# S5 stage of an encoder layer: outputs of a channel tile delayed into the next turn, loops written out, rotations between low parts

## The chip, the cores and the metric

One core of a Trainium2 chip runs the whole program once. The metric is the device time of one execution in microseconds, and what counts is the median of the runs. The engines are PE (TensorE, matmuls), DVE (VectorE), ACT (ScalarE), POOL (GpSimd, here an issuer of DMAs) and SP (SyncE, an issuer of DMAs).

## The reference, cut to what matters

Two layers. Each projects x (256 tokens, 2048 channels) to many parts, runs three mixers on them (an S5 state-space scan with a gate, a Hyena convolution, latent attention), gates and lifts their outputs, projects and normalises. The change touches the S5 mixer, the first steps of attention, and one loop of the lift.

```python
def s5_mixer(u, ...):  # 256 tokens x 1024 channels
    y = uf * d
    for direction in range(2):
        bu = jnp.einsum('blgh,gph->blgp', uf, b_bar)
        _, state = lax.associative_scan(_linear_recurrence_op, (a, bu), axis=1, reverse=(direction == 1))
        y = y + jnp.real(jnp.einsum('blgp,ghp->blgh', state, c_mat))
    y = jax.nn.gelu(y.reshape(bsz, L, W_A))
    return y * jax.nn.sigmoid(y @ w_glu + b_glu)
...
q = (rms_norm(c_q, q_norm_g) @ w_uq).reshape(bsz, L, MLA_HEADS, dqk)
q = jnp.concatenate([q[..., :MLA_NOPE], apply_rope(q[..., MLA_NOPE:], pos)], axis=-1)
k_rope = apply_rope(k_r[:, :, None, :], pos)
```

## The kernel before, in words

**Weights.** All large matmuls run in two parts of fp32r. SP streams 184 blocks of weights (1 MB each) per layer into a ring of four half blocks. For each quarter of a block ACT copies a high part, `WH` (`make_wh`, L398, or `make_wh_quarter`, L404), DVE subtracts it from the raw weights to get the low part, `WL` (`make_wl_quarter`, L417, or `make_wl`, L426), and PE uses both. There is one `WH` and one `WL`, each of four quarters: a quarter can be made anew only when PE has used the old one (`parts_used`). A quarter of `WL` that isn't ready stops PE.

**The S5 stage.** It comes after eight "ax" blocks (the input of the mixer, evicted by ACT, completed by an addition on DVE, `add_input`, L645, sent through `u_scratch` in DRAM and back into `U4` by POOL, 8 DMAs for each of 8 tiles, L476). The stage has 8 turns, one per channel tile `ct`, as a loop (`Fori`) on each engine. PE runs, in a turn, the blocks 0 to 7 of the other projections (`block_at`, `wide_block`, matmuls of lines 1768 and 1770, 16 pairs per block, banks 0 and 1 in turn) and between them five groups of small matmuls:

- after block 1: `turn()` (L1810), transposes of the input matrices `E`, 16 records;
- after block 2: `inputs()` (L1830), 64 records, which need `UC`, the turn's copy of `U4` that ACT makes (L1396);
- after block 3: `lags()` (L1847, L1851), 40 records, which need `F` and `EZ`;
- after block 6: `direct()` (L1866), 16 records, which need `M`, the lags sent through `lag_scratch` by POOL (L488, L494);
- after block 7: `outputs()` (L1887), 64 records, which need the states `SP` that DVE has scanned, and `F`.

ACT evicts the sum of banks 6 and 7 to `Y4` (L1433), POOL sends it through `y_scratch` into `U4` (L498, L506, 8 DMAs). The order of each engine's work is written out by hand: DVE's low parts (`wl_for(j, q)`) and additions (`add_block(j)`, L746) stand between the steps of its own S5 work, ACT's high parts (`split_high(j)`) and evictions (`evict(j)`, L1371) between its own.

**Behind the stage.** ACT squares the latent projections in one instruction (`SQ`, L1439), PE sums them (L1915), ACT makes the eight gelus (L1443), two square roots (L1447), three silus (L1452) and, when PE has run the gate's matmuls (GLU, L1927), eight sigmoids (L1458) that free banks 0 to 3. DVE turns the roots into the normalised latents (L897 to L909), multiplies (L915, L921), and rotates the rotary parts (`rotate`, L927 to L929): that of k after the gate, that of q (4 tiles at once) before the low parts of the second V block. PE goes on with the q projection (L1943, 12 columns), k (8 columns) and V (L1972). The lift of the third branch is a loop of 2 turns of 12 blocks on PE (L2124), with `settle()` (drains that send what releases are pending, L1665) ahead of it and inside each turn.

The matmuls of this stage that wait on others do so by `take_bank` (a bank's last reader is done) and by waits on named semaphores; `ahead=` puts such waits before the last pair of a wide block.

Of the kernel before, what the change touches and what calls it, by code (L numbers as in the profile page):

```python
# [178 lines left out]
def trunk(nc, x, blocks, lp, ln, bc, w1, w2, b3, decay, feats, pT, pos, angles, consts, out):  # L179
    with ExitStack() as ctx:  # L180
# [83 lines left out]
        SQ = area(121, 8)  # L264
# [188 lines left out]
        def _(pool):  # L453
# [7 lines left out]
            for layer in range(DEPTH):  # L461
# [24 lines left out]
                with pool.Fori(0, WT) as ct:  # L486
# [16 lines left out]
                    for q in range(PAIRS):  # L503
                        for g_ in range(2):
                            rows = slice(32 * q + 16 * g_, 32 * q + 16 * g_ + 16)
                            pool.dma_start(split(U4[rows, bass.ds(ct * T, T)], STEP), by_group[q // 2, q % 2, g_]).then_inc(y_loaded, 16)  # L506
# [55 lines left out]
        def _(dve):  # L562
# [61 lines left out]
            for layer in range(DEPTH):  # L624
# [114 lines left out]
                with dve.Fori(0, WT) as ct:  # L739
                    st.enter(ct, DVE_S5_STEPS)  # L740
# [70 lines left out]
                    add_block(1)  # L811
# [76 lines left out]
                    st.leave(WT)  # L888
# [36 lines left out]
                def rotate(x, swapped, n, o):  # L925
                    cb, sb_ = (c.unsqueeze(1).to_broadcast([P, n, T]) for c in (cosr, sinr))
                    st.did(v.tensor_tensor(o, x, cb, ALU.mult))  # L927
                    st.did(v.tensor_tensor(swapped, swapped, sb_, ALU.mult)); st.wait()
                    v.tensor_tensor(o, o, swapped, ALU.add).then_inc(qk_ready, 1)  # L929
# [5 lines left out]
                rotate(PROJt[:, 32:33, :], PROJt[:, 33:34, :], 1, kt[:, 0:1, :])  # L935
# [19 lines left out]
                for i in range(2):  # L955
                    make_wl(dve, v, layer, lift_a(0) if i else B_V + 1)
# [368 lines left out]
        def _(act):  # L1325
# [11 lines left out]
            for layer in range(DEPTH):  # L1337
# [28 lines left out]
                with act.Fori(0, WT) as ct:  # L1366
                    st.enter(ct, ACT_S5_STEPS)
# [58 lines left out]
                    evict(6)  # L1426
                    split_high(7)
                    evict(7)
                    act.wait_ge(y4_free, layer * WT + (ct + 1))
                    for g in range(2):  # L1430
                        full(7 - g, "s5", ct)
                        into = Y4.rearrange("p (q g c) -> p q g c", q=2, g=2)[:, :, g, :]
                        free(a.activation(into, split(bank[7 - g][:, 0:P], 2), ACT.Copy), 7 - g)  # L1433
                    st.leave(WT)

                for b in (0, 1):
                    out_of(b, "s5", 31)

                a.activation(SQ, PROJ[:, 24 * T:32 * T], ACT.Square).then_inc(sq_ready, 1)  # L1439
                act.wait_ge(s_ready, layer * (2 * WT) + 2 * WT)  # L1440
                for ct in range(WT):
                    act.wait_ge(y_loaded, layer * (128 * WT) + 128 * (ct + 1))
# [918 lines left out]
```

## Time and profile before

| | us |
|---|---|
| median of the runs (2472.39, 2474.95, 11741.6) | 2474.95 |
| the profiled execution's own time | 2472.02 |
| its span, first to last instruction | 2470.4 |
| PE busy | 2407.2 |
| PE weight loads busy | 1993.0 |
| DVE busy | 1829.0 |
| ACT busy | 1226.3 |
| POOL busy | 251.2 |

The span is what the rows below divide up: their times run from its start. Layer 0 has its first matmul at 14.73, layer 1 at 1241.57. A matmul's busy time overlaps its neighbour's, so steps between starts tell more than lengths. "issue" is time in which an engine waited for nothing that the profile shows. PEclk is the granted clock of TensorE as a share of 2.4 GHz.

### The profile page before, as it was taken

The numbers are of one execution on the slowest core, as the hardware profiler recorded it, in microseconds if no ns is written. First come the engines' busy times: TensorE is split into PE (matmuls) and PEld (weight loads), VectorE is DVE, ScalarE is ACT, GpSimd is POOL, SyncE is SP. The second block draws the span as 40 slices with busy tenths as digits, with TensorE's granted clock in tenths as the row PEclk, the third lists the DMA queues.
The fourth block names the chain that finished last, engine by engine and source line by source line (L and its number), as shares of the span: only waits on it lengthen the run. The fifth ranks groups of instructions, "written<-read, shape, count | busy, mean of one in ns | idle before, by whom it ended". The sixth has DMA issues, their size and how long they took to land.

```text
span 2470.4 us, 42952 instructions
## 1 busy us (share of the span) xinstructions
PE 2407.2 (97%) x15144; PEld 1993.0 (81%) x15144; DVE 1829.0 (74%) x3195; ACT 1226.3 (50%) x2206; POOL 251.2 (10%) x486
## 2 busy tenths in 40 slices
PE   7999999999999999999989999999999999999998
PEld 6888888887777777898778888888877777788987
DVE  7888888677787776566678888886777777755655
ACT  5555555564543435453455555555654444444534
POOL 3321211100000000000052121121000000000000
PEclk9999999999999999999999999999999999999999
DMA  7555555455453435555565555554544534365553
GB/s 261 186 176 170 178 170 179 150 167 162 154 180 110 150 115 186 192 174 170 170 218 173 170 172 176 176 175 143 172 159 156 177 109 151 117 196 189 171 177 137
DMA packets 124696, 414.72 MB, mean 168 GB/s; under 512 B 19909, under 2 KB 26107, under 8 KB 124337
## 3 DMA queue, kind: packets, MB, share of 16 engines
q1 hardware_dynamic: 107136, 390.12, 47.8%
q0 software_dynamic: 17456, 23.23, 3.3%
q8 instruction: 65, 1.06, 0.2%
q14 instruction: 39, 0.31, 0.1%
HBM read 405.01 MB, written 7.21 MB: 167 GB/s over the span
## 4 chain that ended last, share of the span: by engine, by line
PE 93%; DVE 4%; issue 1%; ACT 1%; PEldq 0%; DMA 0%; PEld 0%; DVEq 0%; POOL 0%; ACTq 0%; POOLq 0%
PE bank L1726 31%; PE bank L1768 21%; PE bank L1770 10%; PE bank L2159 7%; PE bank L1701 5%; PE bank L2079 2%; PE bank L1927 2%; PE bank L1943 2%; PE bank L2093 1%; PE bank L2059 1%; PE bank L1683 1%; PE bank L1999 1%; PE bank L1830 1%; PE bank L1998 1%; PE bank L2041 1%
## 5 line engine op out<-in xcount | busy, mean ns | idle before, releaser
L398 ACT ACTIVATE WH<-ring 128x512 fp32r<-128x512 f32 x1376 | 861.6, 631 | 1105.9 <-PE bank L1726 461.3
L426 DVE TENSOR_TENSOR WL<-ring,WH 128x512 fp32r<-128x512 f32 x860 | 578.3, 689 | 401.1 <-ACT WH L398 398.2
L1768 PE MATMUL bank<-XX,WH 128*128 128x512 f32 x2304 | 830.3, 404 | 31.6 <-DVE XX L617 14.7
L1770 PE MATMUL bank<-XX,WL 128*128 128x256 f32 x2304 | 650.5, 282 | 0.0
L1768 PEld LDWEIGHTS bank<-XX,WH 128*128 128x128 f32 x2304 | 436.0, 189 | 142.4 <-issue 34.1
L1726 PE MATMUL bank<-WH,XX 128*128 128x512 f32 x1536 | 485.8, 398 | 5.0 <-issue 3.0
L417 DVE TENSOR_TENSOR WL<-ring,WH 128x512 fp32r<-128x512 f32 x556 | 380.2, 689 | 149.1 <-ACT WH L398 127.7
L1770 PEld LDWEIGHTS bank<-XX,WL 128*128 128x128 f32 x2304 | 439.6, 191 | 0.0
L1726 PEld LDWEIGHTS bank<-WH,XX 128*128 128x128 f32 x1536 | 285.3, 188 | 81.5 <-issue 21.9
L1726 PE MATMUL bank<-WL,XX 128*128 128x512 f32 x768 | 300.1, 391 | 0.0
L1726 PEld LDWEIGHTS bank<-WL,XX 128*128 128x128 f32 x768 | 144.3, 188 | 30.8
L1701 PE MATMUL bank<-XX,WH 128*128 128x256 f32 x640 | 115.9, 284 | 1.0 <-issue 1.0
L1701 PEld LDWEIGHTS bank<-XX,WH 128*128 128x128 f32 x640 | 99.8, 192 | 1.8 <-issue 1.8
L2159 PE MATMUL bank<-WH,MIXH 128*128 128x512 f32 x256 | 100.5, 393 | 0.0
L2159 PE MATMUL bank<-WL,MIXH 128*128 128x512 f32 x256 | 99.9, 390 | 0.0
L2159 PE MATMUL bank<-WH,MIXL 128*128 128x512 f32 x256 | 99.8, 390 | 0.0
L1701 PE MATMUL bank<-XX,WL 128*128 128x256 f32 x320 | 90.7, 284 | 0.0
L506 POOL DMA_DIRECT2D ARENA<-y_scratch x128 | 66.0, 516 | 81.5 <-DMA y_scratch<-ARENA 63.4
L494 POOL DMA_DIRECT2D ARENA<-lag_scratch x128 | 65.7, 513 | 78.0 <-DMA lag_scratch<-ARENA 52.2
L476 POOL DMA_DIRECT2D ARENA<-u_scratch x128 | 66.5, 528 | 0.2
L1701 PEld LDWEIGHTS bank<-XX,WL 128*128 128x128 f32 x320 | 61.5, 192 | 0.0
L2079 PE MATMUL bank<-ARENA,CON 128*128 128x512 f32 x128 | 57.5, 597 | 0.7 <-issue 0.6
(329 smaller groups left out, 3241.9 us busy)
## 6 DMA issues: line engine op xcount, KB each, us to landing
ring<-in_blocks SPq DMA_DIRECT2D x736, 512.0 KB, 3.3
ARENA<-in_bc POOLq DMA_DIRECT2D x2, 2048.0 KB, 9.0
ARENA<-in_decay POOLq DMA_DIRECT2D x8, 512.0 KB, 4.7
ARENA<-in_x SPq DMA_DIRECT2D x4, 512.0 KB, 7.2
u_scratch<-ARENA POOLq DMA_DIRECT2D x16, 128.0 KB, 3.4
ARENA<-u_scratch POOLq DMA_DIRECT2D x128, 16.0 KB, 3.3
ARENA<-lag_scratch POOLq DMA_DIRECT2D x128, 16.0 KB, 2.7
y_scratch<-ARENA POOLq DMA_DIRECT2D x16, 128.0 KB, 3.4
```

What stands on the lines that cost most here:

```text
L398: nc.scalar.activation(wh[q], raw(which[0], q), ACT.Copy).then_inc(wh_ready[q], 1)
L417: nc.vector.tensor_tensor(wl[q], raw(which[0], q), wh[q].bitcast(F32), ALU.subtract).then_inc(w_used[slot(which[0], q // 2)], 1)
L426: vec.tensor_tensor(wl[q], raw(which[0], q), wh[q].bitcast(F32), ALU.subtract).then_inc(w_used[slot(which[0], half)], 1)
L476: pool.dma_start(split(U4[rows, m * T:(m + 1) * T], 4), by_step[s_, t]).then_inc(u4_loaded, 16)
L494: pool.dma_start(split(M[rows, :], 4), by_half[s_][:, :, (STEP - 1 - t) * 16:(2 * STEP - 1 - t) * 16]).then_inc(m_ready, 16)
L506: pool.dma_start(split(U4[rows, bass.ds(ct * T, T)], STEP), by_group[q // 2, q % 2, g_]).then_inc(y_loaded, 16)
L1701: ins = mm(o, w_, x_, start=start and i == 0 and n == 0, stop=stop and i == 7 and n == 2)
L1726: ins = mm(bank[b][:, :], x_, w_[q], start=first and n == 0, stop=last and n == 2)
L1768: ins = mm(bank[b][:, :], h, xx[:, :, k, :], start=(k == 0), stop=(k == DT - 1), skip_group_check=True)
L1770: ins = mm(bank[b][:, 0:T], l, xh[:, k, :], start=False, stop=(k == DT - 1), skip_group_check=True)
L2079: ins = mm(bank[b][:, :], tab[:, t, m * P:(m + 1) * P], ZT[:, t * W + half * CW:t * W + (half + 1) * CW], start=(t == 0), stop=(t == 1))
L2159: ins = mm(bank[b][:, :], x_[:, k, token[t]], w_[q], start=False, stop=(k == 15 and n == 2), skip_group_check=True)
```

## The change

- PE, ACT, DVE and POOL run the 8 turns of the S5 stage as straight code, not as a loop; so does PE for the lift of the third branch, without its drains.
- On PE, `direct()` and `outputs()` of turn `ct` move into turn `ct + 1`, behind block 1, around `turn()`: direct of the turn before, turn of this one, outputs of the turn before. `inputs()` moves behind block 3, ahead of `lags()`. After the last turn: `direct()`, the sums of squares, `outputs()`.
- The wait for both "ax" additions ahead of the stage and the drains there go.
- ACT: the eviction to `Y4` moves with `outputs()`, behind `turned(1)` of the next turn; `UC` waits for `direct()` of the turn before, and in turn 0 for all U4 loads, not for the first tile's. The squares are eight instructions, four at the end of turn 4 and four at the end of turn 5, into eight scattered areas. The gelus 0 to 2 move ahead of the high parts of the last block.
- DVE: `add_block(1)` moves ahead of the first write of `F`, and that write waits for the matmuls of `outputs()` of the turn before.
- POOL: the y transfer of a turn goes behind block 1 of the next, ahead of its lag transfer.
- DVE: k's rotation goes between low parts of the second k block, q's between the first two low parts of the second V block.

```diff
@@ POOL
-                with pool.Fori(0, WT) as ct:
+                def spread_lags(ct):
...
+                def turn_outputs(ct):
...
+                for ct in range(WT):
+                    if ct:
+                        turn_outputs(ct - 1)
+                    spread_lags(ct)
+                turn_outputs(WT - 1)
@@ DVE
-                with dve.Fori(0, WT) as ct:
-                    st.enter(ct, DVE_S5_STEPS)
+                for ct in range(WT):
...
+                    add_block(1)
                     ft = [b[:, 0:40 * 16] for b in (T1, T2)]
                     for b in (6, 7):
-                        dve.wait_ge(psum_free[b], nth(layer, "s5", b, ct))
+                        if ct:
+                            full(b, "s5", ct - 1)
+                        else:
+                            dve.wait_ge(psum_free[b], nth(layer, "s5", b, ct))
...
-                    add_block(1)
...
-                rotate(PROJt[:, 32:33, :], PROJt[:, 33:34, :], 1, kt[:, 0:1, :])
...
                     make_wl_quarter(q, layer, after_k(4 + q))
+                    if q < 3:
+                        rotate(q, PROJt[:, 32:33, :], PROJt[:, 33:34, :], 1, kt[:, 0:1, :])
...
-                rotate(qr, qs, 4, qt)
+                rotate(0, qr, qs, 4, qt)
+                make_wl_quarter(0, layer, B_V + 1)
+                rotate(1, qr, qs, 4, qt)
+                make_wl_quarter(1, layer, B_V + 1)
+                rotate(2, qr, qs, 4, qt)
@@ ACT
+                def outputs_out(ct):
+                    act.wait_ge(y4_free, layer * WT + (ct + 1))
+                    for g in range(2):
+                        full(7 - g, "s5", ct)
+                        into = Y4.rearrange("p (q g c) -> p q g c", q=2, g=2)[:, :, g, :]
+                        free(a.activation(into, split(bank[7 - g][:, 0:P], 2), ACT.Copy), 7 - g)
...
-                    act.wait_ge(us_landed, layer * WT + WT)
-                    act.wait_ge(u4_loaded, layer * (128 * WT) + (ct * 128 + 128))
-                    a.activation(UC, U4[:, bass.ds(ct * T, T)], ACT.Copy).then_inc(uc_ready, 1)
+                    if ct == 0:
+                        act.wait_ge(us_landed, layer * WT + WT)
+                        act.wait_ge(u4_loaded, layer * (128 * WT) + 128 * WT)
+                    if ct:
+                        act.wait_ge(direct_done, layer * (2 * WT) + 2 * ct)
+                    a.activation(UC, U4[:, ct * T:(ct + 1) * T], ACT.Copy).then_inc(uc_ready, 1)
                     turned(0)
                     turned(1)
+                    if ct:
+                        outputs_out(ct - 1)
...
                     evict(6)
+                    if ct == WT - 1:
+                        act.wait_ge(s_ready, layer * (2 * WT) + 2 * WT)
+                        for k in range(3):
+                            gelu(k)
                     split_high(7)
                     evict(7)
...
+                    if 4 <= ct < 6:
+                        if ct == 4:
+                            for b in (0, 1):
+                                out_of(b, "s5", 15)
+                        for k in range(4 * ct - 16, 4 * ct - 12):
+                            a.activation(SQ[k], PROJ[:, (24 + k) * T:(25 + k) * T], ACT.Square).then_inc(sq_ready, 1)
+                outputs_out(WT - 1)
+                for k in range(3, WT):
+                    gelu(k)
...
-                a.activation(SQ, PROJ[:, 24 * T:32 * T], ACT.Square).then_inc(sq_ready, 1)
@@ PE
-                settle()
                 pe.wait_ge(consts_loaded, 16)
-                with pe.Fori(0, WT) as ct:
+                for ct in range(WT):
...
-                    for b in (0, 1):
-                        out_of(b, "ax", 3)
+                    def all_made():
+                        matrices_made()
+                        if ct:
+                            lags_spread(ct - 1)
+                            states_made(ct - 1)
                     block_at(0)
-                    block_at(1, matrices_made)
+                    block_at(1, all_made)
+                    if ct:
+                        direct()
                     turn()
-                    block_at(2, matrices_turned)
+                    if ct:
+                        outputs(ct - 1)
+                    block_at(2)
+                    block_at(3, matrices_turned)
                     inputs()
-                    block_at(3)
                     lags()
                     block_at(4)
                     block_at(5)
-                    block_at(6, lags_spread)
-                    direct()
-                    block_at(7, states_made)
-                    outputs()
+                    block_at(6)
+                    block_at(7, (lambda: lags_spread(WT - 1)) if ct == WT - 1 else None)
+                direct()
                 for i in range(2):
-                    pe.wait_ge(sq_ready, layer + 1)
+                    pe.wait_ge(sq_ready, layer * 8 + (4 * i + 4))
...
+                    if i == 0:
+                        states_made(WT - 1)
+                outputs(WT - 1)
...
-                settle()
-                with pe.Fori(0, 2) as turn:
-                    for j in range(12):
-                        if j == 4:
-                            pe.wait_ge(yl_ready, layer * 4 + 4)
-                        gated_block("lift", j // 6 + turn * 2, j % 6, (xh, xl), yb, B_LIFT + 48 + j, turn, 12)
-                    settle()
+                for j in range(24):
+                    if j == 4:
+                        pe.wait_ge(yl_ready, layer * 4 + 4)
+                    gated_block("lift", j // 6, j % 6, (xh, xl), yb, B_LIFT + 48 + j)
```

## Rows read from the trace of the kernel before

**Rows 1.** The page, part 1: busy us, share of the span, instructions
```profile
PE 2407.2 (97%) x15144; PEld 1993.0 (81%) x15144; DVE 1829.0 (74%) x3195; ACT 1226.3 (50%) x2206; POOL 251.2 (10%) x486
```

**Rows 2.** Waits of PE: for whom, total us, times, longest us
```profile
PE bank L1915 <- ACT ARENA L1439: 5.9, 2, 2.9
PE bank L1768 <- issue: 4.9, 14, 0.5
...
PE bank L1768 <- DVE ARENA L645: 4.2, 2, 2.1
PE bank L1726 <- issue: 3.0, 4, 0.9
...
PE bank L1943 <- DVE WL L417: 1.3, 2, 0.7
```

**Rows 3.** PE timeline around turn() and inputs(): start us, us, instruction, count, idle before
```profile
435.37 0.40 PE L1768 MATMUL bank<-XX,WH 128*128 128x512 f32 x1
435.61 0.28 PE L1770 MATMUL bank<-XX,WL 128*128 128x256 f32 x1
435.82 0.71 PE L1810 MATMUL bank<-CON,ARENA 64*128 64x64 f32 x16
436.46 0.50 PE L1768 MATMUL bank<-XX,WH 128*128 128x512 f32 x1
...
442.31 1.16 PE L1830 MATMUL bank<-ARENA 64*64 64x64 f32 x64
```

**Rows 4.** PE timeline, the first s5 block of layer 0
```profile
70.19 0.49 PE L1768 MATMUL bank<-XX,WH 128*128 128x512 f32 x1 [2.10 <-DVE ARENA L645]
```

**Rows 5.** Windows behind two idle times: us, five engines busy, PEclk, DMA share, GB/s
```profile
478.30:481.70 3.40, 3.40 (x9) 2.72 (x9) 0.42 (x1) 3.39 (x7) 1.21 (x3) 0.50 0.10 37
1294.10:1297.50 3.40, 3.40 (x12) 2.84 (x11) 1.08 (x3) 0.63 (x1) 3.40 (x8) 0.50 0.69 234
```

**Rows 6.** POOL's U4 loads of layer 0's end and to landing; a turn's y loads
```profile
72.51 8.06 POOL L476 DMA_DIRECT2D ARENA<-u_scratch  x16
...
DMA to landing us min/median/max: 1.9/3.3/4.2
...
278.40 5.12 POOL L506 DMA_DIRECT2D ARENA<-y_scratch  x8 [4.51 <-DMA y_scratch<-ARENA]
```

**Rows 7.** ACT timeline in turn 0 of layer 0, from the UC copy on
```profile
82.59 0.41 ACT L1396 ACTIVATE ARENA<-ARENA 128x256 f32 x1
...
84.91 1.22 ACT L398 ACTIVATE WH<-ring 128x512 fp32r<-128x512 f32 x2
```

**Rows 8.** ACT timeline from the last outputs to the sigmoids of layer 0
```profile
486.76 0.66 ACT L1443 ACTIVATE ARENA<-ARENA 128x256 f32<-128x256 f32 x1 [4.06 <-DMA ARENA<-y_scratch]
...
504.02 1.28 ACT L1458 ACT_TABLE_LOAD   x1
508.07 3.43 ACT L1458 ACTIVATE ARENA<-bank,PAR 128x256 f32<-128x256 f32 x8 [2.77 <-PE bank L1927]
```

**Rows 9.** PE timeline over the same stretch
```profile
477.59 5.41 PE L1915 MATMUL bank<-ARENA,CON 128*128 128x256 f32 x16 [2.94 <-ACT ARENA L1439]
482.83 1.46 PE L1927 MATMUL bank<-ARENA,ring 128*128 128x256 f32 x6
...
510.27 0.47 PE L1943 MATMUL bank<-CH,WH 128*128 128x256 f32 x1
```

**Rows 10.** Timeline, turn 4 of layer 0: first low part for block 7, its start
```profile
313.53 0.68 DVE L417 TENSOR_TENSOR WL<-ring,WH 128x512 fp32r<-128x512 f32 x1
315.68 0.50 PE L1768 MATMUL bank<-XX,WH 128*128 128x512 f32 x1
```

**Rows 11.** Code loads (packets, MB, share) in the loop, in straight code; the latter's window
```profile
q8 instruction: 1, 0.02, 0.0%
...
q8 instruction: 8, 0.13, 0.2%
...
560.00:800.00 240.00, 239.24 (x1014) 180.63 (x1012) 183.15 (x345) 111.75 (x193) 4.06 (x8) 1.00 0.47 152
```

More of the change, by code:

```diff
@@ L261, in trunk @@
         YAH, YAL, SIG = parts("YAH", 73, 8), parts("YAL", 81, 8), area(89, 8)
-        SQ = area(121, 8)
+        SQ = [area(at, 1) for at in (107, 108, 109, 110, 111, 97, 115, 129)]
         RS = area(113, 2)
@@ L887, in _ @@
                     st.wait()
-                    st.leave(WT)
                 for b in (6, 7):
@@ L923, in _, with rotate @@
                 cosr, sinr = ROPE[:, 0:T], ROPE[:, T:2 * T]
-                def rotate(x, swapped, n, o):
+                def rotate(step, x, swapped, n, o):
                     cb, sb_ = (c.unsqueeze(1).to_broadcast([P, n, T]) for c in (cosr, sinr))
-                    st.did(v.tensor_tensor(o, x, cb, ALU.mult))
-                    st.did(v.tensor_tensor(swapped, swapped, sb_, ALU.mult)); st.wait()
-                    v.tensor_tensor(o, o, swapped, ALU.add).then_inc(qk_ready, 1)
+                    if step == 0:
+                        st.did(v.tensor_tensor(o, x, cb, ALU.mult))
+                    elif step == 1:
+                        st.did(v.tensor_tensor(swapped, swapped, sb_, ALU.mult))
+                    else:
+                        st.wait()
+                        v.tensor_tensor(o, o, swapped, ALU.add).then_inc(qk_ready, 1)
                 kt = tiles(KT, 0, 4)
@@ L1363, in _, with gelu @@
                 act.wait_ge(tanh_ready, layer * 3 + 3)
-                with act.Fori(0, WT) as ct:
-                    st.enter(ct, ACT_S5_STEPS)
+                def outputs_out(ct):
[4 more added lines that the diff above has]
+                        free(a.activation(into, split(bank[7 - g][:, 0:P], 2), ACT.Copy), 7 - g)
+                def gelu(k):
+                    act.wait_ge(y_loaded, layer * (128 * WT) + 128 * (k + 1))
+                    a.activation(Ut[:, k, :].rearrange("p (c t) -> p c t", t=STEP),
+                                 U4[:, k * T:(k + 1) * T].rearrange("p (t c) -> p c t", t=STEP), ACT.Gelu_apprx_tanh).then_inc(gelu_ready, 1)
+                for ct in range(WT):
                     def evict(j):
@@ L1426, in _ @@
                     evict(6)
+                    if ct == WT - 1:
+                        act.wait_ge(s_ready, layer * (2 * WT) + 2 * WT)
+                        for k in range(3):
+                            gelu(k)
                     split_high(7)
                     evict(7)
[L1429 to L1434, printed above, removed]
-                for b in (0, 1):
-                    out_of(b, "s5", 31)
-                a.activation(SQ, PROJ[:, 24 * T:32 * T], ACT.Square).then_inc(sq_ready, 1)
-                act.wait_ge(s_ready, layer * (2 * WT) + 2 * WT)
-                for ct in range(WT):
-                    act.wait_ge(y_loaded, layer * (128 * WT) + 128 * (ct + 1))
-                    a.activation(Ut[:, ct, :].rearrange("p (c t) -> p c t", t=STEP),
-                                 U4[:, ct * T:(ct + 1) * T].rearrange("p (t c) -> p c t", t=STEP), ACT.Gelu_apprx_tanh).then_inc(gelu_ready, 1)
+                    if 4 <= ct < 6:
[7 more added lines that the diff above has]
+                    gelu(k)
                 for i in range(2):
@@ L1786, in _ @@
                     wide_block(m % 2, B_AX + m)
-                settle()
                 pe.wait_ge(consts_loaded, 16)
-                with pe.Fori(0, WT) as ct:
+                for ct in range(WT):
                     part_of = lambda buf, r, d, q, w: buf[:, (r * 8 + d * PAIRS + q) * w:(r * 8 + d * PAIRS + q + 1) * w]
@@ L1852, in lags, with lags_spread @@
                         done(ins, 4)
-                    def lags_spread():
+                    def lags_spread(ct):
                         pe.wait_ge(m_ready, layer * (128 * WT) + (ct * 128 + 128))
```

14 lines of the change are left out of this document (8 added, 6 removed).

## The prediction

> **What bounds the kernel now.** I read the page first: PE is busy 97% of the span, DVE 74%, ACT 50% [rows 1]. So the time is PE's stream of matmuls plus what stands between them, and only the stream's own gaps and small steps can give time back. Then the waits of PE [rows 2]: 63 us of idle time in all, of which the change touches five groups. The reader is to see that each is small, and that two of them (the squares of L1439 and the last addition of L645) are one long wait in each layer. Then the timeline of PE inside the S5 stage: sixteen turns (8 in each layer) of eight wide blocks and five groups of small matmuls. A block is 5.65 us: from the start of one at 436.46 to the next group at 442.31 there are 5.85, of which 0.10 is the slow first matmul (0.50 long, where one inside the stream is 0.40) and 0.09 the slow step into the group (0.21 where a step inside the stream is 0.12) [rows 3].
>
> **The change part by part.** The profiled execution took 2472.0 us beside a span of 2470.4; the median of the runs shown is 2474.95, so I count from 2472.0 and leave 3 us of spread to the range.
>
> *Straight code in place of the loops (A).* PE's return in the S5 loop costs 0.35 us of idle time, 14 times: 4.9 gone. The lift loop's four (entry and return, two layers): 3.0 gone [rows 2]. Sum 7.9. What straight code may cost is the last rival.
>
> *Fewer ways into small matmuls (B).* turn() has 16 records in 8 steps (two run at once), 0.71 us; inputs() 64 in 16 steps (four at once), 1.16 [rows 3]. So a step is 0.45/8 = 0.056, and the 8 steps of turn() are 0.45. From the last wide matmul before it (435.61) to the first behind it (436.46) pass 0.85. Less the steps (0.45) and the ordinary step between wide ones (0.12), plus the slow first matmul (0.10), the way in and out costs 0.38, whatever is inside. Before, a layer has 8 x 5 = 40 such ways. After, turns 1 to 7 have two (direct, turn, outputs together; inputs and lags together), turn 0 two, and the tail two (direct; outputs): 18. That is 22 fewer in a layer. But where one group hands over to another, something stays: at least nothing, at most the 0.19 that is neither the step in nor the slow wide matmul; a full 0.38 if a handover is as dear as a way out and in. No row shows such a handover. I take 0.17 kept, 0.21 saved, near the 0.19, since every handover here also changes the shape (64*128, 64*64, 128*32): 44 x 0.21 = 9.2, bounds 0 and 16.7. The Trainium skill, TensorEngine Tiling (Array Packing), Key Properties, says that changing the tiling mode, not just the tile, drains TensorE; by it the handovers keep their cost, as I take it, and without it B would be near its upper bound.
>
> *The first block of the stage (C).* Before, PE waits for the last addition before the whole stage: 2.10 and 2.12 us of idle time [rows 2, 4]. That wait (and the drains ahead of the loop) go: block 0 needs bank 0 alone, freed one addition earlier, and bank 1 is wanted 5.65 us later. 4.2 gone. In layer 1 the granted clock stands at 0.50, 1.2 GHz, for 3.4 us just behind that idle time [rows 5]; at full clock the same work takes 1.7. Together 5.9.
>
> *The inputs' landing (D), a new wait.* In turn 0 ACT's copy into UC now waits for all 64 loads of U4, not for the first tile's 8. The last is issued at 72.51 + 8.06 - 0.50 = 80.07 and lands a median 3.3 later: 83.4 [rows 6]. The copy began at 82.59 [rows 7] with PE's stage from 70.19 [rows 4]; with PE 2.1 earlier it would begin at 80.5, so it is 2.9 late against PE. Queued behind it on ACT are the two evictions of turn(), four small copies and the high parts of block 3, which were made from 84.91 [rows 7]; now from 85.7, the first ready at 86.3, its low part (0.68 on DVE [rows 10]) at 87.1. PE gets there at 68.1 + 3 x 5.65 + 0.85 = 85.9, since inputs() no longer lies before block 3. PE waits 1.2 to 1.4 in each layer: 2.6 lost. Bounds: 0 if the loads land 1.9 after issue, 4.0 if they land 4.2 after. POOL, bound by its own issue rate here, isn't helped by an earlier PE.
>
> *The delayed steps in turns 1 to 7.* outputs() of the turn before needs states that were ready in block 7 and lags spread by DMA some 20 us before; nothing is late. On DVE the write of F now waits for outputs(), which ends some 2.2 us behind block 1; the high and low part of block 2's last quarter (0.63 + 0.68 and the semaphores) and the addition moved ahead of it take as long. UC waits for direct(), half a microsecond behind block 1, while ACT is at its last high part. The two evictions of outputs into Y4 move from the end of a turn to ahead of block 3's high parts, where ACT still is ahead of PE by over a microsecond. On POOL the y transfers now go ahead of the lags' and end about when LAG is evicted. I cost all this at nothing; the cover is thinnest before block 7 (third rival).
>
> *The tail of the stage (E).* The wait for the squares, 2 x 2.94, goes (they are made in turns 4 and 5), and so does the half clock behind it: 3.4 us at 0.50 in each layer, 1.7 each [rows 5]. 9.3 gone. What is late next: the sigmoids of the gate, which free the banks that the q projection takes. Before, outputs ended at 477.59 - 2.94 = 474.65 [rows 9] and ACT was ready for the sigmoids at 504.02 + 1.28 = 505.30, 30.65 later, behind the y transfer and the last gelu (486.76) [rows 8]; then it idled 2.77 for PE. Between outputs and GLU lay the squares' matmuls; now they lie ahead of outputs. So GLU, 27.44 long (482.83 to 510.27) [rows 9], follows outputs at once. ACT's chain isn't shorter, but for POOL's issues: 8 in a loop took 5.12, 16 in straight code 8.06, so 1.1 less [rows 6]. PE's banks are free 30.65 - 1.1 + 0.86 (two of eight sigmoids in 3.43 [rows 8]) + 0.2 = 30.6 behind outputs; GLU ends at 27.5. A new wait of 3.1 in each layer: 6.2, and as it is longer than the one that brought the half clock, 3.4 for that again. Net -0.3. Gelus 0 to 2 ahead of it gain nothing: they were never last.
>
> *The rotations (F).* The one of k goes behind the low parts that PE waited for (L1943, 1.3 in all [rows 2]); the one of q lets two low parts of the V block through. 1.3 gone.
>
> Sum: 7.9 + 9.2 + 5.9 - 2.6 - 0.3 + 1.3 = 21.4. 2472.0 - 21.4 = 2451.
>
> **Rivals.**
> 1. *The sigmoids are not late.* For it: the whole chain hangs on one DMA round trip and on table loads. Against it: 2.77 us of slack against some 8 that the move of outputs takes away. Then E is 9.3: 2441.
> 2. *A handover costs a full way.* For it: none is shown. Against it: the slow wide matmul can't recur. B is 0: 2460.
> 3. *The low parts are late at block 7.* Before, the first is done at 314.21 and PE starts at 315.68 [rows 10], 1.5 ahead; direct() no longer lies before block 7, which takes 0.8 of it. DVE has no idle time there. If as much again is missing, some 0.7 a turn, 14 turns: 10 lost, 2461.
> 4. *Slower than before: PE runs out of code.* In the loop a code load comes once in 290 us; in straight code 8 come in 240 us, for 2,026 records of PE, 253 to a load [rows 11]. Fourteen turns of 912 records (8 blocks of 64, 400 in small groups) need about 50 loads. A stretch of direct, turn and outputs passes 192 of these in 2 us; POOL's loads need 1.9 at the least to land [rows 6]. With 1.0 us exposed each, 50: 2501. It is slower than before from 0.43 a load on. Against it: the straight stretch is 239.24 of 240 busy. The Trainium skill, Advanced Engine Details and Errata, ISA Cache, gives TensorE 128 KB of instructions in lines of 256; the trace agrees that the loop stays and that straight code loads by such pieces.
>
> **How the numbers follow.** Forecast 0.60; rivals in turn 0.14, 0.11, 0.10 and 0.05. The forecast's own range is 2443 to 2459, from B's and D's bounds at half their reach. Taking in rivals 1 to 3 and 3 us between executions: 2432 to 2466; above lies rival 4, below only B at its upper bound with rival 1. Over 2% faster would be below 2422.6, which is beyond all terms at their best but a few: 0.03. Over 2% slower, above 2521.4, needs most of rival 4: 0.02. Within 2%, which is about what a measurement of this kernel can tell from no change: 0.95.
>
> **What would show it.** A turn of 49.5 to 49.8 us in place of 50.7; no "issue" waits at L1768 and L1726; no wait at the squares' matmuls; one idle time of 1 to 1.5 us at block 3 of turn 0, released by a low part; one of about 3 us at the q projection, released by a sigmoid, with PEclk 0.50 behind it. Wrong if waits for low parts stand in every turn, if the sum of the small groups' time doesn't fall, or if the q projection starts without a wait.

## The result and the profile after

The changed kernel takes 2446.97 us (median of 3 runs, 2443.91 to 2446.97), 0.989 of the kernel before (95% interval 0.9876 to 0.9904): within 2%, and clearly less than before, by some 27 us. Measured again with the experiments it takes 2445.94 us, 0.9888 [0.9872, 0.9905]. Its profiled execution took 2446.97 us beside a span of 2445.2, so between the two profiled executions the span fell by 25.2 us. The forecast was 2451.

Here is the first part of the profile's page, as in [rows 1], and the code loads of TensorE's queue (packets, MB, share). PE has lost 13 us of busy time with the same number of instructions:

```profile
PE 2394.5 (98%) x15144; PEld 1990.7 (81%) x15144; DVE 1820.4 (74%) x3195; ACT 1225.0 (50%) x2220; POOL 248.8 (10%) x486
...
q8 instruction: 120, 1.97, 0.3%
```

The waits of PE after, as in [rows 2] (for whom, us in total, times, longest us). The stage's matmuls are now L1806 and L1808, the q and k projection is L1990, the lift L1764. Gone are the "issue" waits at the stage, the entry wait for the last addition and the wait for the squares; new are a late low part at the stage (L417) and the sigmoids (L1496). At the lift 0.7 us of "issue" is left of 3.0, and its wait for low parts (L426) is longer, 3.6 for 1.9:

```profile
PE bank L1806 <- DVE XX L626: 15.1, 1, 15.1
...
PE bank L1806 <- DVE WL L426: 5.7, 4, 3.6
PE bank L1806 <- DVE WL L417: 4.1, 2, 2.2
PE bank L1764 <- DVE WL L426: 3.6, 4, 1.6
...
PE bank L1990 <- ACT ARENA L1496: 1.5, 2, 0.8
...
PE bank L1764 <- issue: 0.7, 2, 0.3
...
PE bank L1990 <- DVE WL L417: 0.2, 1, 0.2
```

PE's timeline over one turn's new group, as in [rows 3]: start us, us, instruction, count. The three small groups stand between two wide matmuls, at 1441.35 and 1443.90, and the next turn's direct() comes 49.68 us after this one's (before: a turn of 50.45 to 50.82):

```profile
1441.11 0.40 PE L1806 MATMUL bank<-XX,WH 128*128 128x512 f32 x1
1441.35 0.28 PE L1808 MATMUL bank<-XX,WL 128*128 128x256 f32 x1
1441.55 0.68 PE L1903 MATMUL bank<-ARENA 64*64 64x64 f32 x16
1442.17 0.71 PE L1847 MATMUL bank<-CON,ARENA 64*128 64x64 f32 x16
1442.81 1.16 PE L1924 MATMUL bank<-ARENA 64*64 64x64 f32 x64
1443.90 0.50 PE L1806 MATMUL bank<-XX,WH 128*128 128x512 f32 x1
```

Turn 0 of layer 0. First the loads of U4 on POOL, as in [rows 6], then ACT from its wait for them on, as in [rows 7] (start us, us, instruction, count, idle before):

```profile
72.83 8.06 POOL L476 DMA_DIRECT2D ARENA<-u_scratch  x16
```

```profile
80.29 0.37 ACT L1406 ACTIVATE ARENA<-bank 128x256 f32<-128x256 f32 x1
84.33 0.42 ACT L1434 ACTIVATE ARENA<-ARENA 128x256 f32<-128x256 f32 x1 [3.67 <-DMA ARENA<-u_scratch]
84.65 1.07 ACT L1411 ACTIVATE ARENA<-bank 128x512 f32<-128x512 f32 x2
85.61 1.02 ACT L1418 ACTIVATE ARENA<-ARENA 64x128 f32<-64x128 f32 x4
86.66 1.15 ACT L398 ACTIVATE WH<-ring 128x512 fp32r<-128x512 f32 x2
```

What PE makes of it, and the window behind it with the granted clock, as in [rows 5] (us, the five engines' busy times, clock, DMA share, GB/s): block 3 starts 2.15 us late, and the next 3.4 us run at half clock.

```profile
88.16 0.77 PE L1806 MATMUL bank<-XX,WH 128*128 128x512 f32 x1 [2.15 <-DVE WL L417]
88.72 0.41 PE L1808 MATMUL bank<-XX,WL 128*128 128x256 f32 x1
```

```profile
88.10:91.50 3.40, 3.35 (x11) 2.89 (x12) 3.35 (x6) 3.40 (x9) 0.00 (x0) 0.50 0.48 155
```

The tail of layer 0: PE, as in [rows 9] (L1903 direct, L1959 squares' sums, L1924 outputs, L1974 GLU, L1990 q projection). There is no idle time before the sums, and 0.72 us before the q projection:

```profile
467.71 0.68 PE L1903 MATMUL bank<-ARENA 64*64 64x64 f32 x16
468.32 3.72 PE L1959 MATMUL bank<-ARENA,CON 128*128 128x256 f32 x16
471.97 1.16 PE L1924 MATMUL bank<-ARENA 64*64 64x64 f32 x64
473.06 1.13 PE L1974 MATMUL bank<-ARENA,ring 128*128 128x256 f32 x4
...
501.68 0.35 PE L1990 MATMUL bank<-CH,WH 128*128 128x256 f32 x1 [0.72 <-ACT ARENA L1496]
```

The two ends of ACT's chain over the same stretch, as in [rows 8], and POOL's y transfer of the same outputs:

```profile
499.29 1.28 ACT L1496 ACT_TABLE_LOAD   x1
500.58 3.03 ACT L1496 ACTIVATE ARENA<-bank,PAR 128x256 f32<-128x256 f32 x8
```

```profile
474.09 0.56 POOL L501 DMA_DIRECT2D y_scratch<-ARENA  x1 [18.36 <-ACT ARENA L1394]
476.66 4.04 POOL L509 DMA_DIRECT2D ARENA<-y_scratch  x8 [2.01 <-DMA y_scratch<-ARENA]
```

### The profile page after: what moved, and what is told of

The parts are those of the page before. It is cut to its first block, busy times and chain, and to the rows that moved or that the text cites. A ratio compares the mean times of both kernels' runs of the same rounds, so it can differ in the third digit from the quotient of the medians.

```text
span 2445.2 us, 40924 instructions
## 1 busy us (share of the span) xinstructions
PE 2394.5 (98%) x15144; PEld 1990.7 (81%) x15144; DVE 1820.4 (74%) x3195; ACT 1225.0 (50%) x2220; POOL 248.8 (10%) x486
## 3 DMA queue, kind: packets, MB, share of 16 engines
q8 instruction: 120, 1.97, 0.3%
## 4 chain that ended last, share of the span: by engine, by line
PE 89%; POOL 3%; DVE 3%; ACT 2%; issue 2%; DMA 1%; DVEq 0%; POOLq 0%; ACTq 0%
PE bank L1764 32%; PE bank L1806 19%; PE bank L1808 10%; PE bank L2203 7%; PE bank L1739 5%; POOL ARENA L476 3%; PE bank L2126 2%; PE bank L1990 2%; PE bank L2140 1%; PE bank L2106 1%; PE bank L1721 1%; PE bank L2019 1%; PE bank L2046 1%; PE bank L1924 1%; PE bank L1867 1%
## 5 line engine op out<-in xcount | busy, mean ns | idle before, releaser
L426 DVE TENSOR_TENSOR WL<-ring,WH 128x512 fp32r<-128x512 f32 x856 | 575.0, 689 | 399.7 <-ACT WH L398 397.2
L1806 PE MATMUL bank<-XX,WH 128*128 128x512 f32 x2304 | 825.0, 402 | 27.4 <-DVE XX L626 15.1
L1808 PE MATMUL bank<-XX,WL 128*128 128x256 f32 x2304 | 649.8, 282 | 0.0
L1806 PEld LDWEIGHTS bank<-XX,WH 128*128 128x128 f32 x2304 | 436.1, 189 | 137.7 <-issue 27.5
L1764 PE MATMUL bank<-WH,XX 128*128 128x512 f32 x1536 | 485.0, 397 | 4.3 <-DVE WL L426 3.6
L417 DVE TENSOR_TENSOR WL<-ring,WH 128x512 fp32r<-128x512 f32 x560 | 380.7, 687 | 138.1 <-ACT WH L398 119.2
L1808 PEld LDWEIGHTS bank<-XX,WL 128*128 128x128 f32 x2304 | 438.6, 190 | 0.0
L1764 PEld LDWEIGHTS bank<-WH,XX 128*128 128x128 f32 x1536 | 285.2, 188 | 79.8 <-issue 17.9
L1764 PE MATMUL bank<-WL,XX 128*128 128x512 f32 x768 | 299.8, 390 | 0.0
L1764 PEld LDWEIGHTS bank<-WL,XX 128*128 128x128 f32 x768 | 144.1, 188 | 31.0
```

Source lines behind the costliest of these rows:

```text
L417: nc.vector.tensor_tensor(wl[q], raw(which[0], q), wh[q].bitcast(F32), ALU.subtract).then_inc(w_used[slot(which[0], q // 2)], 1)
L426: vec.tensor_tensor(wl[q], raw(which[0], q), wh[q].bitcast(F32), ALU.subtract).then_inc(w_used[slot(which[0], half)], 1)
L1764: ins = mm(bank[b][:, :], x_, w_[q], start=first and n == 0, stop=last and n == 2)
L1806: ins = mm(bank[b][:, :], h, xx[:, :, k, :], start=(k == 0), stop=(k == DT - 1), skip_group_check=True)
L1808: ins = mm(bank[b][:, 0:T], l, xh[:, k, :], start=False, stop=(k == DT - 1), skip_group_check=True)
```

## The experiments

Twelve runs: three on the kernel before, each with one part of the change, and nine of or on the changed kernel. The intervals of neighbouring ratios overlap in most cases, so what an edit of 2 or 3 us does is read from the trace, and the medians only have to agree. One thing moves them beside the edits: a run of wide matmuls has two paces, 5.65 or 5.55 us a block, and which one it has differs from kernel to kernel (last section). "Short" below means the second.

**The changed kernel beside the first three.**

> The changed kernel once more, beside the next three. From its earlier runs: 0.989 of the kernel before, about 2447 us. Each run beside it is read as a difference to this one.

Measured: 2445.94 us, 0.9888 [0.9872, 0.9905], span 2444.2.

**Wait for the first tile alone (D).**

```diff
-pool.dma_start(split(U4[rows, m * T:(m + 1) * T], 4), by_step[s_, t]).then_inc(u4_loaded, 16)
+pool.dma_start(split(U4[rows, m * T:(m + 1) * T], 4), by_step[s_, t]).then_inc(u4_loaded if m else u4_first, 16)
...
-                        act.wait_ge(u4_loaded, layer * (128 * WT) + 128 * WT)
+                        act.wait_ge(u4_first, layer * 128 + 128)
+                    if ct == 1:
+                        act.wait_ge(u4_loaded, layer * (128 * (WT - 1)) + 128 * (WT - 1))
```

> The changed kernel, with ScalarE's first copy of an input tile waiting for the eight loads of that tile alone (a semaphore of their own); the other 56 are waited for in turn 1. Theory: in the changed kernel this copy stands behind the last U4 load, which lands at 84.2 us where PE's first block began at 68.3, and everything that ScalarE does for the ring behind it is late: PE idles 2.15 us before block 3 of turn 0 in layer 0 and is at half clock for 3.4 us behind it (block of 7.06 for 5.64 us, so 1.4), and idles about 2.0 us in layer 1. All of that goes: -5.6 us, near 2441.4, and the trace shows no wait over 0.3 us for the low parts in turn 0 and full clock from 80 to 95 us. Rival 1: ScalarE's own work at the start of the stage, or VectorE's, is too long for PE in turn 0 whatever it waits for: the wait stays, within 0.5 us of the changed kernel. Rival 2: the wait moves to turn 1's block, as ScalarE has the same loads to wait for there: they have landed 40 us before, so I give it little; it would be -1 to 0.

Measured: 2441.33 us, 0.987 [0.9854, 0.9887], span 2438.0. Its list of PE's waits has none at the stage for that low part, and the window of turn 0 in which the changed kernel shows a clock of 0.89 is busy from end to end:

```profile
80.00:95.00 15.00, 15.00 (x191) 12.81 (x190) 12.99 (x21) 10.92 (x25) 1.91 (x4) 1.00 0.60 198
```

Blocks 2 and 3 of turn 0 take 15.34 us in the changed kernel (layer 0; 13.56 in layer 1) and 11.51 here (11.30 in layer 1). The theory holds: the wait costs 3.8 + 2.1 = 5.9 us against a run of 11.50, and both rivals fall. In the changed kernel's other trace, the one beside this run, it is 15.74 and 12.59, so 5.3. Medians: 4.6 less, spans: 6.2 less. Not all of that is the wait: here turn 0's long run and all eight runs of two blocks of layer 1 are short, which is worth 0.6 + 8 x 0.2 = 2.2 us, and layer 0 reaches turn 0's block 2 some 1.0 us later.

**Outputs ahead of the sums (E).**

```diff
                 direct()
+                states_made(WT - 1)
+                outputs(WT - 1)
                 for i in range(2):
                     pe.wait_ge(sq_ready, layer * 8 + (4 * i + 4))
...
-                    if i == 0:
-                        states_made(WT - 1)
-                outputs(WT - 1)
```

> The changed kernel, with the last tile's outputs ahead of both sums of squares behind turn 7 (they stand behind them), and VectorE's first read of the sums waiting for the second one too. Theory: the chain outputs, their write to y_scratch, its return as U4, gelus, table load, sigmoids is what the q projection waits for (0.72 us each layer); it starts 3.65 us earlier, so that wait goes: -1.4 us, near 2445.5. Rival: the last states are not ready when PE wants them without the first sum (1.8 us) in front: PE waits up to 1.8 us there in each layer and at most the clock's loss besides, 0 to +2.2 us.

Measured: 2443.72 us, 0.9878 [0.9862, 0.9895], span 2443.3: 2.2 less by the medians, 0.9 by the spans. No wait for a sigmoid is left in PE's list. From GLU's start (473.50) to the q projection (500.94) pass 27.44 us, as before the change (482.83 to 510.27, [rows 9]); in the changed kernel it is 28.62 (473.06 to 501.68). So the late sigmoids cost 1.2 us in each layer, more than the 0.72 that stands as idle time. The states are not late; the idle time that is left is a wait of outputs() for PE's own direct():

```profile
467.99 0.68 PE L1905 MATMUL bank<-ARENA 64*64 64x64 f32 x16
468.86 1.16 PE L1926 MATMUL bank<-ARENA 64*64 64x64 f32 x64 [0.19 <-PE bank L1905]
```

**Both.**

> Both edits of the two runs before this one. If the waits of turn 0 and of the tail are independent their gains add: -7.0 us, near 2440. If the second edit brings a wait for the states, -3.5 to -5.6, near 2442.5.

Measured: 2439.58 us, 0.9861 [0.9844, 0.9877], span 2437.5. The gains nearly add (6.4 less than the changed kernel by the medians; 4.6 + 2.2 alone), and neither wait is in PE's list, so the two are independent.

**The entry wait alone (C), on the kernel before.**

```diff
-                    for b in (0, 1):
-                        out_of(b, "ax", 3)
                     block_at(0)
```

> The kernel before, without PE's wait at the start of the stage for ScalarE's read of banks 0 and 1 (the block takes each bank by its own wait). Theory: the idle 2.10 us ahead of the first block goes in both layers (4.2) and the half clock behind it in layer 1 with it (1.7): -5.9 us, 0.9976 of before. Rival 1: the banks' own waits, or a low part that is not ready, end at the same moment and PE idles as before: 0. Rival 2: PE comes earlier, but turn 0's later blocks then wait for the low parts, as in the changed kernel: half of it is given back, -2 to -3.

Measured: 2465.3 us beside 2472.96, 0.9967 [0.9954, 0.9979], span 6.7 less. The half clock at 1294 us is gone, and neither rival shows. By the steps from a layer's first matmul to block 2 of turn 0 the entry gives 1.6 us in layer 0 (67.39 to 65.78) and 3.1 in layer 1 (65.63 to 62.54), 4.7 and not 5.9: PE still idles 0.47 and 0.45 us there, released by nothing that the profile shows. The drains of settle(), which stay in this run, stand at this place. But the loop gave too, and the list says where: the "issue" waits at L1768 fell from 4.9 us in 14 to

```profile
PE bank L1768 <- issue: 1.9, 7, 0.5
```

and two of these 7 are the ones at the entry. The two waits stood inside the loop, so PE passed them in each turn, long met: from the last outputs() to the first wide matmul of the next turn were 1.50 us (1445.61 to 1447.10 in the trace of before), here 1.31; over the 14 turns it is 2.7 less. Beside that, 11 of the 14 runs of two blocks behind a return are short here and 5 before, 1.2 us that the edit may not have made.

**The stage's loop alone (A), on the kernel before.**

```diff
-                with pe.Fori(0, WT) as ct:
+                for ct in range(WT):
```

> The kernel before, with PE's eight turns of the stage written out instead of a loop (PE's only; the other engines' loops stay). Theory: each of the 14 returns costs PE 0.35 us and code of eight turns is fetched ahead without a stall: -4.9 us, 0.998. Rival 1: the returns are hidden behind work already queued on PE: 0, 1.000. Rival 2: straight code has to be loaded by PE as it goes, and PE waits for it about 0.25 us at each load, 3 to 4 in a turn: +8 or more. The count of code packets and PE's idle without a releaser tell them apart.

Measured: 2465.57 us beside 2472.96, 0.9974 [0.9965, 0.9983]. The same step is 1.09 here:

```profile
1444.18 1.16 PE L1887 MATMUL bank<-ARENA 64*64 64x64 f32 x64
1445.27 0.50 PE L1768 MATMUL bank<-XX,WH 128*128 128x512 f32 x1
```

So this return cost 0.40 us (1.50 - 1.09), 0.19 of it the two waits inside the loop (they stand in the straight code too, where they cost nothing that shows), and the 14 together 5.9. The rest of the 7.4 us by the medians goes with the pace: all 14 runs of two blocks are short here, 9 more than before, 1.8 us. The page counts 116 code packets where the loop had 65, and PE's list has no "issue" wait at the stage: straight code of this length is fetched without a stall. Rivals 1 and 2 fall.

**The lift's loop alone, on the kernel before.**

```diff
-                settle()
-                with pe.Fori(0, 2) as turn:
-                    for j in range(12):
...
+                for j in range(24):
+                    if j == 4:
+                        pe.wait_ge(yl_ready, layer * 4 + 4)
+                    gated_block("lift", j // 6, j % 6, (xh, xl), yb, B_LIFT + 48 + j)
```

> The kernel before, with the loop of two turns in the lift stage written out and its two settles gone. Theory: the settles and the return cost 1.5 us each layer: -3.0 us, 0.9988. Rival: they stand beside waits for low parts or for the banks that stay: 0 to -1.

Measured: 2470.36 us beside 2472.96, 0.999 [0.9981, 0.9999]. All "issue" waits at L1726 go (3.0), and waits for low parts there grow from 1.9 to

```profile
PE bank L1726 <- DVE WL L426: 3.7, 4, 1.7
```

By the list that is a net 1.2 us, and 1.0 more of "issue" at L1701. The steps give more: from the last matmul ahead of the lift's 24 blocks to the first behind them (L2093 to L1701) pass 138.08 us in each layer, 139.92 and 139.90 before, and 0.1 less behind that: 3.8 in all, over the theory's 3.0. The medians show less of it (2.6). This trace has a half clock of 3.4 us at 72.52, in a part that the edit doesn't touch, which before doesn't have. It also places the changed kernel's 3.6 us at L1764: they come with the straight lift, not with the rotations.

**inputs() behind block 2 again (B).**

```diff
                     block_at(2)
-                    block_at(3, matrices_turned)
                     inputs()
+                    block_at(3)
```

(with matrices_turned moved to block 2.)

> The changed kernel, with inputs() behind block 2 again (in the changed kernel it stands ahead of lags(), behind block 3). It adds one way out of the wide matmuls and back in each of 16 turns and takes one handover between small groups away. Theory (way 0.38 us, handover 0.16 to 0.20): +0.2 in each turn, +3.2 us, 0.9900 of before if the changed kernel is 0.9887. Rival 1: a handover is free and only the way counts: +6.1, 0.9912. Rival 2: neither costs, and the gain of the joining came from elsewhere: 0. Rival 3: the turned matrices are not ready that much earlier (5.6 us), and PE waits for them: a new wait in its list and more than +6.

Measured: 2445.28 us, 0.9888 [0.9873, 0.9903], the changed kernel's ratio: the total says "neither costs". The trace says otherwise. A turn is 49.78 us here (49.68), but its two blocks run as 5.85 and 5.75 (block 2 from 1442.47 to 1448.32). Split at one pace they are 2 x 5.85 = 11.69 against 11.50 together: a way saved (one exit from the wide matmuls and one return) is worth 0.20 us, as the theory had it, and inputs() itself takes 1.09 whoever follows it. Of that, 0.10 is lost to the pace of wide matmuls (below). And turn 0 gives 2 us back: with inputs() ahead of block 3 the late low part is waited for 1.2 us in all, not 3.4 as in the changed kernel beside the first three, and one wait of 1.1 us for ScalarE's copy of the turned matrices is what is left of rival 3.

**The rotations undone (F).**

```diff
-                    if q < 3:
-                        rotate(q, PROJt[:, 32:33, :], PROJt[:, 33:34, :], 1, kt[:, 0:1, :])
...
+                for step in range(3):
+                    rotate(step, PROJt[:, 32:33, :], PROJt[:, 33:34, :], 1, kt[:, 0:1, :])
```

(and q's rotation likewise.)

> The changed kernel with both rotations in one piece again, as in the kernel before: k's ahead of the low parts of the next stage, q's ahead of them too. Theory: PE's waits for low parts in q/k projection come back, 1.3 us in both layers together, and nothing else moves: +1.3 us. Rival: the rotations between the low parts only moved the wait to the V stage (its waits for low parts went from 1.9 to 3.6 us): then they go back too and the sum is 0 or a little below.

Measured: 2447.97 us, 0.9898 [0.9884, 0.9912], 2.0 over the changed kernel. Two waits come back, and the lift's doesn't go:

```profile
PE bank L1763 <- DVE WL L426: 3.7, 4, 1.7
...
PE bank L1989 <- DVE WL L417: 1.3, 2, 0.7
PE bank L2018 <- DVE WL L417: 1.0, 2, 0.5
```

1.3 - 0.2 + 1.0 = 2.1. The rival falls.

**turn() first.**

```diff
+                    turn()
                     if ct:
                         direct()
-                    turn()
-                    if ct:
                         outputs(ct - 1)
```

> The changed kernel with turn() ahead of direct() and outputs(): direct() and outputs(), both of 64-row forms, then stand next to each other, and the number of groups is the same. Theory: what a handover costs hangs on the change of tile form between the groups: direct to outputs takes 0 and 14 handovers of 0.16 to 0.20 go: -2.5 us. Rival 1: it hangs on the groups' own first matmul (its wait or its load), whatever the form: 0. Rival 2: turn() earlier by 0.6 us, or direct() later, meets a wait: up to +3.

Measured: 2438.56 us, 0.9867 [0.9852, 0.9881], span 2436.0. That is more than any theory gave, and not by its mechanism. From direct() to outputs(), the pair of one form, it takes 0.78 us where direct() to turn() took 0.61 (outputs() waits for direct()'s own semaphore, as in the second experiment), so 0.16 is lost. Whether a change of form costs anything stays open. The gain is in the wide matmuls. PE's groups by line, from one lags() to the next small group; first the changed kernel, 1457.00 to 1491.23:

```profile
L1806 PE MATMUL bank<-XX,WH 128*128 128x512 f32 x96 | 34.1, 400 | 0.0
L1808 PE MATMUL bank<-XX,WL 128*128 128x256 f32 x96 | 27.0, 281 | 0.0
```

and turn() first, 1450.80 to 1484.41:

```profile
L1806 PE MATMUL bank<-XX,WH 128*128 128x512 f32 x96 | 33.4, 392 | 0.0
L1808 PE MATMUL bank<-XX,WL 128*128 128x256 f32 x96 | 26.9, 280 | 0.0
```

The same 192 matmuls, no wait in either, clock 1.00 in both, and 34.11 us against 33.49: a pair takes 353.5 or 347 ns. All 14 such runs of six blocks are of the short kind here, none in the changed kernel. 14 x (0.63 - 0.16) = 6.5 us, and turn 0's wait brought no half clock in this execution, 1.7 more. Together that is 8.2, the size of the difference between the two spans (2444.2 and 2436.0).

**The squares at the end of turn 7 (E).**

```diff
-                    if 4 <= ct < 6:
-                        if ct == 4:
+                    if ct == WT - 1:
...
-                        for k in range(4 * ct - 16, 4 * ct - 12):
+                        for k in range(8):
```

> The changed kernel with ScalarE's eight squares of the latents at the end of turn 7 instead of four each in turns 4 and 5. Theory: they end after PE wants the sums, as in the kernel before (idle 2.94 us there and half clock behind): +2.9 in each layer and 1.7 for the clock, +5.9 to +9.3 us. Rival: the sums now come later behind direct(), by then the squares are made, and the gain of the tail came from the order alone: 0.

Measured: 2453.85 us, 0.9918 [0.9905, 0.9931], 7.9 over the changed kernel. The wait is back, shorter than in [rows 9], and the sums take 5.4 us for 3.7:

```profile
471.07 5.41 PE L1958 MATMUL bank<-ARENA,CON 128*128 128x256 f32 x16 [1.86 <-ACT ARENA L1477]
...
471.00:474.50 3.50, 3.43 (x10) 2.76 (x11) 0.19 (x1) 1.24 (x5) 0.00 (x0) 0.61 0.86 279
```

2 x (1.86 + 1.7) = 7.1, and the waits for the late low part at turn 0 are 5.3 us here for 3.4 to 4.1. The theory holds; moving the squares to turns 4 and 5 is what removed this wait, and the order of sums and outputs did not.

**All three edits.**

> The changed kernel with three edits: ScalarE's first copy waits for the first tile's loads alone, the last outputs stand ahead of the sums of squares (both as in the pair measured before: 2439.6 us), and turn() stands ahead of direct() and outputs(). The last edit alone gave 7.4 us; its trace puts 0.63 us of each of 14 turns on the run of six blocks (33.49 for 34.11 us: each pair of wide matmuls at 347 for 353.5 ns) and gives 0.16 back where outputs() waits for direct() just ahead of it. Theory: the fast pace belongs to the order turn, direct, outputs: 2439.6 - 14 x 0.45 = 2433.3 us, turns of 49.23 us. Rival: the pace follows from the moment at which the run starts, which the other edits shift, so that it may fall back to 353.5 ns and only the 0.16 stays: 2441.8 us, turns of 49.8 us.

Measured: 2433.3 us (5 runs, 2431.7 to 2435.4), 0.9837 [0.9824, 0.9851]. From turn 2 of layer 0 on every turn with outputs is 49.23 us, and 12 of the 14 runs of six blocks are short. The median is the theory's to the tenth, with two runs that kept the slow pace, as the rival has it for all: so the order decides most of the runs and something else the other two. This is the fastest version: 12 to 14 us under the changed kernel.

## Why the prediction was right

The verdict (within 2%), the range and the forecast's direction held; 2451 was 4 us above the median. The sum was 21.4 against 25.2 between the spans, and that it came so near was luck in part: E gave 7.2 us more than forecast, D cost 3.3 more, and the two met.

- *A, straight code, 7.9.* Held: 5.9 at the stage (4.9 forecast) and 3.8 at the lift (3.0 forecast; the changed kernel has the same 138.08 us there as the run with the lift alone). One thing was not seen: the long-met waits inside the loop are part of each return.
- *B, fewer ways, 9.2.* Held, by its own reasoning: the 0.19 that belongs to the wide side (slow step in, slow first matmul) is what is saved, 0.20 measured, and what belongs to the small group stays at a handover. In the rows of one turn's new group 2.55 us pass from 1441.35 to 1443.90; less 1.80 for the steps and 0.12 for the ordinary one, plus 0.10, that is 0.73, a way of 0.38 and two handovers of 0.17. A regular turn of the straight kernel before is 50.05 us, the changed one's 49.68; at equal pace of the wide runs the difference is 0.57, which is three ways at 0.19.
- *C, the entry, 5.9.* Held in kind, 5.0 in size. Both idle times went, and what PE spent there beside them: from a layer's first matmul to block 2 of turn 0 it is 67.39 us before and 64.94 after in layer 0, 65.63 and 63.10 in layer 1. Layer 1's half clock at 1294 went, but another of 3.4 us stands at 1234.98, behind an idle time of 1.91 us among the ax blocks; before, the same idle time (1.90, up to 1246.85) brought none. So layer 1 gained 2.5 and not 3.8.
- *D, the inputs' landing, -2.6.* The mechanism held, the size failed: 5.9 in this trace, and 3.7 to 7.2 in the others that have this wait and inputs() behind block 3. Two terms were mis-sized. The last load was issued at 80.38 and the copy that waits for all of them began at 84.33, where 83.4 was forecast (the median landing was taken for the last of 64, which needed some 3.8 here); with it block 3 was 2.15 late and not 1.2 to 1.4. And the half clock, which the prediction charged to the idle times at the tail, was not charged here: 3.4 us at 0.50, 1.7.
- *E, the tail, +9.3 - 9.6.* The first half held; the second was the step that failed most. A sigmoid wait of 3.1 with half clock was forecast; it costs 1.2 a layer, at full clock. From the end of outputs (471.97 + 1.16 = 473.13) to the end of the table load (499.29 + 1.28 = 500.57) are 27.44 us, not 30.65 - 1.1 = 29.55. The chain is not fixed: the write to y_scratch took from 474.09 to its landing at 476.08, 2.0 us; before, it was issued at 475.92, 0.55 behind a ring load, and landed at 479.39, 3.5. The 14 traces of this case say what goes with that: 210 of these writes were issued 0.2 to 0.6 us behind a ring load and took 3.2 to 4.5 us, the 14 that were not took 2.0. With the last outputs ahead of the sums these writes fall 0.47 behind one and take 4.1 and 4.0 again. That the ring load is the cause was not tried by itself. The remaining 0.6 is an issue that comes 0.96 behind outputs for 1.27, and 0.3 around the loads. With 9.3 gone and 2.4 lost, E is 6.9. So rival 1 (the sigmoids are not late, 2441) was half true.
- *F, the rotations, 1.3.* Held, and 2.1 in size: a second wait for low parts went too, that of the V blocks. It stood in PE's list of before, and the prediction gave it no price:

```profile
PE bank L1972 <- DVE WL L426: 1.2, 2, 0.6
```

- *The delayed steps at nothing.* Held. ACT and DVE stay ahead of PE in turns 1 to 7; rival 3 (low parts late at block 7) fell, though the margin there (the block's first low part done, its start) went from 1.46 us down to 0.76, by what was forecast. Rival 2 (a handover costs a full way) fell by B, rival 4 (PE runs out of code) by the 120 packets without an "issue" wait at the stage.

Of the signs that were named, the turn of 49.5 to 49.8 us and the missing waits at the stage and the squares came; the idle time at block 3 was 2.15 us for 1 to 1.5, and the one at the q projection 0.72 for 3, without a half clock.

With the measured sizes (B as 44 x 0.19 = 8.4): 5.9 + 3.8 + 8.4 + 5.0 - 5.9 + 6.9 + 2.1 = 26.2. In the kernel before 5 of 14 runs of two blocks are short (11.29 for 11.50, below), in the changed one none, which takes 1.0 back: 25.2, as between the spans, where small things that no term has (the first matmul comes 0.4 us later, F is 0.4 more by the steps) cancel.

The Trainium skill, TensorEngine Tiling (Array Packing), Key Properties, says that a change of tiling mode drains TensorE. The prediction weighed it as a cost of each handover. The trace shows that 0.17 us stays with each small group; no run here shows that the form is the cause, since the one pair of equal form met a wait of its own.

## What to carry to other kernels

Where an engine is 97% busy, add up the small things that come back in every turn: a loop's return together with the long-met waits at its head (0.4 us), and a break in the stream of wide matmuls (0.20 us, however small the group in it). When a wait is widened from one tile's loads to all, price it with a slow landing of the last load, with all that stands behind the waiting instruction, and with the half clock that an idle time of 2 us may bring; count by tile where a semaphore costs nothing. And when steps are delayed past the end of a loop, look whether the last one heads a long chain, and let that one go first.

## What the runs showed of the hardware that was not expected

The stream of wide matmuls (512 columns, then 256) has two paces at the same granted clock. Single steps in the long pace go 232, 118, 241, 120, 235, 114 ns and again, 353.5 a pair; in the short pace 230, 117, 347 a pair. A run keeps the pace it began with, and over the 14 long runs of a kernel it is nearly always the same: 34.11 us in all of the changed kernel's (in both of its traces), 33.49 in all of the kernel with turn() first and in 12 of 14 of the one with all three edits. The order of the small groups ahead is not all that decides: with the order unchanged, turn 0 of layer 0 has the short pace in the run that waits for the first tile alone, and its runs of two blocks take 11.49 to 11.51 us in layer 0 and 11.30 in all of layer 1, by the same code. With the rotations undone, an edit behind the stage, layer 0 has the 11.30 from turn 1 on and layer 1 the 11.49. Some phase between what feeds PE and PE itself would fit; it wasn't tried. The pace is worth 0.6 us in 34, 8.8 us over the stage's long runs, more than most edits here, so a difference of a few us between two orders of the same work should be looked for in the steps between matmuls before it is put down to the edit.

The half clock followed idle times of 2 us unevenly. At turn 0 of the changed kernel it came behind the 2.15 us in layer 0 and not behind the 1.93 us in layer 1; in the kernel with turn() first (2.02 and 1.28) in neither layer, and with the outputs ahead of the sums not even behind 2.99 us. At the entry it came behind 1.97 us in the kernel before with straight turns (layer 0), and not behind 2.10 us in the kernel before itself.
